# Splits of activations and norms of compressed inputs queued at other places beside the products, in a two-block transformer kernel on one core

## What is computed

```python
# first block, after the mixer
x = x + m[2] * rms_norm(y, norm_mix_post)
f = swiglu(modulate(rms_norm(x, norm_ffn_pre), m[3], m[4]), w_gate, w_up, w_down)
x = x + m[5] * rms_norm(f, norm_ffn_post)
...
# second block, each of two layers
h = rmsnorm(h_res, norm_gain[l])
proj = h @ w_in[l]            # u_pool, z_pool, c_q, c_kv, k_rope, z_mla, g_pool, g_mla
y_pool = (pool_mix(u_pool) * silu(z_pool)) @ pool_w_up[l]
c_q, c_kv = rmsnorm(c_q, g_qa), rmsnorm(c_kv, g_kva)    # 768 and 256 wide
o_mla = attention(c_q @ w_q_b, c_kv @ w_kv_b, k_rope)
y_mla = (o_mla * silu(z_mla)) @ mla_w_up[l]
merged = sigmoid(g_pool) * y_pool + sigmoid(g_mla) * y_mla
h_res = h_res + merged @ w_out[l]
```

## Time and profile before

| | |
|---|---|
| time, median of 3 runs | 3752.34 us (3749.4 to 3755.61) |
| the profiled execution | 3751.09 us, its span 3749.3 us |
| PE busy | 3390.0 us, 90% |
| DVE, ACT, POOL busy | 1957.6, 1434.3, 218.8 us |
| mean granted TensorE clock | 0.936 of full |
| chain that ended last | PE 77%, DVE 14%, ACT 6%, issue 1%, DMA 1% |
| DMA | 321.82 MB, mean 86 GB/s |

### The profile page before, as it was taken

The page is one execution under the profiler, slowest core; times in us unless marked ns, Lnnn a source line. Parts: engine busy times, 40 slices in busy tenths (PEclk is TensorE's granted clock), DMA queues, the critical chain, the costliest instruction groups (busy, mean ns, idle before and its releaser), DMA issues.

```text
span 3749.3 us, 51094 instructions
## 1 busy us (share of the span) xinstructions
PE 3390.0 (90%) x20406; PEld 2828.6 (75%) x20406; DVE 1957.6 (52%) x2838; ACT 1434.3 (38%) x2196; POOL 218.8 (6%) x225
## 2 busy tenths in 40 slices
PE   1998776579999999998998999999999989999998
PEld 1776544467778777878855779999988557799998
DVE  6647577866544444446454544454453645444433
ACT  2532465334432333234245443342342444433322
POOL 1000033210000000000020000000000200000000
PEclk9999876569999999999999999999999989899999
DMA  5562101013333224222200002333432000033333
GB/s 194 181 204 92 46 17 62 3 66 112 107 112 118 94 92 158 96 96 103 81 1 29 24 24 88 108 131 94 136 109 75 1 29 24 24 88 107 116 91 102
DMA packets 94493, 321.82 MB, mean 86 GB/s; under 512 B 10352, under 2 KB 11632, under 8 KB 93488
## 3 DMA queue, kind: packets, MB, share of 16 engines
q1 hardware_dynamic: 76224, 249.66, 20.3%
q0 software_dynamic: 17312, 67.78, 5.1%
q10 hardware_dynamic: 720, 1.12, 0.1%
HBM read 295.38 MB, written 23.20 MB: 85 GB/s over the span
## 4 chain that ended last, share of the span: by engine, by line
PE 77%; DVE 14%; ACT 6%; issue 1%; DMA 1%; DVEq 0%; ACTq 0%; POOL 0%; SPq 0%; POOLq 0%
PE psum L146 74%; DVE mixer L171 4%; PE psum L149 3%; DVE mixer L181 2%; DVE wlo L171 1%; DVE arena L171 1%; DVE junk L185 1%; ACT arena L155 1%; DVE arena L194 1%; ACT whi L163 1%; DVE mixer L198 1%; ACT arena L154 1%; DVE region L171 1%; ACT arena L163 0%; ACT region L163 0%
## 5 line engine op out<-in xcount | busy, mean ns | idle before, releaser
L146 PE MATMUL psum<-region,whi 128*128 128x260 f32 (+2 forms) x8896 | 1909.6, 312 | 28.8 <-DVE region L171 22.3
L146 PEld LDWEIGHTS psum<-region,whi 128*128 128x128 f32 (+1 forms) x8896 | 1443.6, 188 | 138.8 <-issue 28.8
L146 PE MATMUL psum<-region,wlo 128*128 128x260 f32 (+2 forms) x4448 | 1380.2, 310 | 0.0
L171 DVE TENSOR_TENSOR wlo<-stage,whi 128x1024 fp32r<-128x1024 f32 (+2 forms) x454 | 512.7, 1129 | 777.1 <-ACT whi L163 742.1
L146 PEld LDWEIGHTS psum<-region,wlo 128*128 128x128 f32 (+1 forms) x4448 | 839.6, 189 | 49.2
L163 ACT CAST whi<-stage 128x1024 fp32r<-128x1024 f32 (+2 forms) x454 | 441.8, 973 | 272.2 <-PE psum L146 172.8
L146 PE MATMUL psum<-arena 128*128 128x65 f32 (+8 forms) x2064 | 419.5, 354 | 4.1 <-ACT arena L155 2.3
L163 ACT COPY arena<-psum 128x512 f32<-128x512 f32 (+10 forms) x428 | 190.0, 444 | 431.3 <-PE psum L146 397.2
L146 PE MATMUL psum<-mixer 64*128 64x128 f32 (+6 forms) x1140 | 228.5, 443 | 122.5 <-DVE mixer L171 56.3
L146 PEld LDWEIGHTS psum<-arena 128*128 128x128 f32 (+4 forms) x2064 | 253.7, 180 | 101.1 <-issue 90.5
L154 ACT ACTIVATE arena<-psum 128x260 f32<-128x260 f32 (+1 forms) x236 | 100.8, 427 | 598.7 <-PE psum L146 598.0
(11 more groups left out here) (144 smaller groups left out, 2796.4 us busy)
## 6 DMA issues: line engine op xcount, KB each, us to landing
stage<-in_w SPq DMA_DIRECT2D x144, 512.0 KB, 3.5
stage<-in_wi SPq DMA_DIRECT2D x55, 512.0 KB, 4.2
stage<-in_wm SPq DMA_DIRECT2D x48, 512.0 KB, 3.4
stage<-in_wo SPq DMA_DIRECT2D x48, 512.0 KB, 3.4
stage<-in_wg SPq DMA_DIRECT2D x44, 512.0 KB, 3.2
stage<-in_wu SPq DMA_DIRECT2D x44, 512.0 KB, 3.2
stage<-in_wd SPq DMA_DIRECT2D x32, 512.0 KB, 3.3
arena<-xr_scratch POOLq DMA_DIRECT2D x7, 2080.0 KB, 9.1
```

The costliest lines, as they stand in the source:

```text
L146: return Issued(self, self.e and self.e.matmul(out, w, x, start=start, stop=stop, skip_group_check=True))
L171: return Issued(self, e and e.tensor_tensor(out, a, b, op))
```

## The change

It does these things:

- `Halves` can wait for its place row by row (`room(k)`). `h_second` waits for row k of the narrow product instead of the whole one (`pe_gemm` signals each row, `each=True`); `h_mg` waits for its first four rows only for the last but one up product, and DVE makes these four ahead of the last up product's four instructions.
- `hf[0]` waits for the first chunk's last output product, and is queued in the last two steps of the output stage, on DVE between the last four scalings.
- `hf[1]` and `h_in[0]` are steps beside the third part's down products, two per product, no longer at once ahead of them; the squares of the last norm (`END1`) follow them.
- The norm of the compressed inputs of half 0 is queued after `h_second`, beside the second half's products; that of half 1 goes in one product earlier; both have four empty steps before the roots, not two.
- The norms of layer 1's input have other empty steps: `steps(3, 3, 2)` for `(0, 1, 0)` and `steps(9, 6, 0)` for `(7, 4, 0)`.

```diff
-def pe_gemm(e, W, bank, psum, key, name, units, rhs, nch, N, done, count, M=128):
+def pe_gemm(e, W, bank, psum, key, name, units, rhs, nch, N, done, count, M=128, each=False):
...
                 ins = e.matmul(o, wl[:, k, :], xh, False, n == len(units) - 1 and k == nk - 1)
+                if each and ci == nch - 1 and k < nk - 1:
+                    ins.then_inc(*done.up("row", key, k))
             if ci < nch - 1:
...
                 done.mark(key, ci)
+                if each and ci == nch - 1:
+                    done.mark("row", key, nk - 1)
...
 def stages(n, s):
...
     def __init__(self, key, st, hi, lo, src, ready, free, B=None):
-        self.key, self.st, self.hi, self.lo, self.src, self.ready, self.free, self.B = (
-            key, st, hi, lo, src, ready, free, B)
+        self.key, self.st, self.hi, self.lo, self.src, self.ready, self.B = key, st, hi, lo, src, ready, B
+        self.room = free if callable(free) else lambda k: free
...
     def steps(self):
...
 def act_half(e, h, k):
     A = h.st.act
-    for c, s in (*h.ready(k), *h.free):
+    for c, s in (*h.ready(k), *h.room(k)):
         e.wait_ge(*c[s])
...
 def dve_half(e, h, k):
     A, D = h.st.act, h.st.dve
-    for c, s in (*h.ready(k), *h.free):
+    for c, s in (*h.ready(k), *h.room(k)):
         e.wait_ge(*c[s])
...
     hf = [Halves(f"f{ch}", sout, fh, fl, nx[ch], lambda k, ch=ch: [(sout.dve, ("sc", ("pre", ch), k))],
-                 [(sout.pe, (("wo", 1, 7), 0))] if ch == 0 else [(sffn.pe, (("wu", 0, 21), 0))],
+                 [(sout.pe, (("wo", 0, 7), 0))] if ch == 0 else [(sffn.pe, (("wu", 0, 21), 0))],
                  B=mod[:, 24:32]) for ch in range(2)]
...
     LAY0 += n_in[1].scales()
-    END1 = [x for s in n_end1[0].squares() for x in (*GAP, s)]
+    sq = n_end1[0].squares()
+    END1 = [sq[0], sq[1], sq[2], *GAP, *GAP, *GAP, sq[3]]
...
     OUT1 += [added(n_post[0][0], "post", 0, xc, n_pre[0])[a:b] for a, b in ((2, 7), (7, 14), (14, 21))]
-    OUT1 += [[], [("root", n_pre[0], 0), ("rec", n_pre[0], 0)], n_pre[0].scales(), []]
+    sc, hv = n_pre[0].scales(), hf[0].steps()
+    OUT1 += [[], [("root", n_pre[0], 0), ("rec", n_pre[0], 0)], sc[0:4], [x for k in range(4) for x in (hv[k], sc[4 + k])] + hv[4:]]
...
-    def half_now(e, q, h):
-        for k in range(8):
+    def half_now(e, q, h, k0=0, k1=8):
+        for k in range(k0, k1):
             if q == "act":
...
                 bs.flush()
-        half_now(e, "act", hf[0])
...
     def dve_out(e, bs):
...
                 bs.flush()
-        half_now(e, "dve", hf[0])
...
     def pool_out(e, bs):
...
                         lambda ci, k_: (uh[:, k_], ul[:, k_], D["ul", ch, k0 + k_]), 1, 512, T, A if part == 0 else D)
-                bs.tick()
+                bs.tick(2 if part == 2 else 1)
         T.mark("end" if ch else "half")
...
     def act_ffn(e, bs, ch, mid):
...
                     e.copy(yc[ch][:, m], psum[:, bank.of[key, 0], :]).then_inc(*A.up(key, 0))
-                bs.tick()
+                bs.tick(2 if part == 2 else 1)
...
     def dve_ffn(e, bs, ch, mid):
...
                         *D.up(key, 0))
-                bs.tick()
+                bs.tick(2 if part == 2 else 1)
...
     def ffn(q, f, e, bs):
...
             def mid():
                 bs.flush()
-                half_now(e, q, h_in[0] if ch else hf[1])
-                bs.todo += END1 if ch else []
+                bs.todo += (h_in[0] if ch else hf[1]).steps() + (END1 if ch else [])
             f(e, bs, ch, mid)
...
                        (lambda k: [(S1.dve, ("sc", ("next", 1, 1), k))]),
-                       [(slay[l].pe, (("kr", l, 0), 1))]) for l in range(2)]
-    LAYER = [LAY0, n_in1[1].steps(7, 4, 0)]
+                       lambda k, l=l: [(slay[l].pe, ("row", ("kr", l, 0), k))]) for l in range(2)]
+    LAYER = [LAY0, n_in1[1].steps(9, 6, 0)]
...
     def n_lora(l, half):
...
                     lambda k, l=l, half=half: [(slay[l].dve, (("up", l, half, k, 1), 1))],
-                    [(slay[l].pe, (("up", l, half, 7, 1), 1))]) for half in range(2)] for l in range(2)]
+                    lambda k, l=l, half=half: [(slay[l].pe, (("up", l, half, 7, k // 4), 1))])
+             for half in range(2)] for l in range(2)]
     POOLS = [[s for g, wnd in enumerate((2, 4, 8, 16)) for s in
...
+    def lora_steps(l, half):
+        q_, kv_ = LORA[l][half]
+        out = q_.squares() + kv_.squares() + 4 * GAP + [("root", q_, 0), ("root", kv_, 0)]
+        return out + [("rec", q_, 0), ("rec", kv_, 0)] + q_.scales() + kv_.scales()
...
     def rounds(l, half, e, bs, q, do):
...
                     slay[l].act.mark("tail", l, half)
+            if (n, half) == (7, 1):
+                bs.todo += lora_steps(l, 1)
             bs.tick(4)
-            if n == 7:
-                q_, kv_ = LORA[l][half]
-                bs.todo += q_.squares() + kv_.squares() + 2 * GAP + [("root", q_, 0), ("root", kv_, 0)]
-                bs.todo += [("rec", q_, 0), ("rec", kv_, 0)] + q_.scales() + kv_.scales()
         if half == 0:
...
             half_now(e, q, h_second[l])
+            bs.todo += lora_steps(l, 0)
         else:
...
             def do(key, i):
                 if key[0] == "kr":
-                    pe_gemm(e, W, bank, psum, key, f"wk_{l}", [i], rhs, 2, HC, T, A, M=32)
+                    pe_gemm(e, W, bank, psum, key, f"wk_{l}", [i], rhs, 2, HC, T, A, M=32, each=True)
                 else:
...
         elif l == 0:
-            out += n_in1[0].steps(0, 1, 0)
+            out += n_in1[0].steps(3, 3, 2)
         return out
...
     def beside3(l, half):
...
                 dve_weights(e, W, W.last[key] + 2)
+                if (k, z) == (7, 1):
+                    bs.flush()
+                    half_now(e, "dve", h_mg[l][half], 0, 4)
                 for ci in range(2):
...
         bs.flush()
-        half_now(e, "dve", h_mg[l][half])
+        half_now(e, "dve", h_mg[l][half], 4)
         bs.todo += beside3(l, half)
...
             key = ("wo2", l, half, k)
```

## The result

| | before | changed |
|---|---|---|
| time, median of 4 runs each | 3752.69 us (3749.4 to 3755.61) | 3727.88 us (3724.8 to 3728.76) |
| the profiled execution, its span | 3751.09, 3749.3 us | 3728.76, 3727.0 us |
| mean granted clock | 0.936 | 0.936 |

What follows compares the result with a forecast made beforehand. PE, busy 90% of the span, bounds the kernel, so only its waits or low clock cost time. Terms -19.5 -5.1 -1 -3.6 -3.4 +4 = -28.6 from 3751.1 give 3722.5, 1.2 more against the median: 3723 us, range 3708 to 3737.

Steps and rivals of the forecast that it cites:

- Compressed norms, -19.5: Four norms of the compressed inputs: PE's 3.8 us waits before the column sums go and the sums run faster, saving 19.5 us.
- the 11.4 us against 13.6: Behind the compressed norms' sums, reciprocals and weight split end after 11.4 us; PE has work for 13.6, so they stay hidden.
- Split of half 1, layer 0, -5.1 and 0 for the row-wise release: Second token half: layer 0 becomes like layer 1, saving 5.1 us; freeing each row by itself gives 0 in both layers.
- Merged halves, -1: Four splits of the merged rows: DVE ends no sooner, PE waits twice; 1 us gained in all, through the clock.
- The rule weighed there: At the merged halves, shorter waits may leave the clock high at all four sites, giving up to 10 us instead of 1.
- Halves inside the FFN, -3.6: Third part of the down products: halves fit beside the products, removing PE's waits of 2.20 and 1.39 us; 3.6 us saved.
- Input norms of layer 1, -3.4: Column sums of layer 1's two input norms: 2 us saved at the first, about 2 us wait remaining, and 1.4 at the second.
- FFN start, +4: First FFN split: four scalings between the halves make row 7 3.1 us later, plus 0.9 for the clock; 4 us lost.
- the bounds of parts 3, 5 and 6: Merged halves: gain 2.5 to loss 1.5 us a site; first layer-1 input norm: 0 to 4 saved; FFN start: 3 to 6 lost.
- row by row works: Rival: merged halves end near PE's pace, 5.7 us at each of four sites, some 5 at two half changes; 3682 to 3712; chance 0.11.
- A new wait: Rival: PE stalls 3.5 us behind the reciprocals at each of four norms, 14 us in all; 3737 us; chance 0.10.
- slower: Rival: products beside the norms wait 2.2 us for weights, 20 times, 44 us; 3767 us; chance 0.02.

Runs made afterwards that it cites:

- norms alone: Only the compressed-input norms moved, with four empty steps, on the kernel before: 3732.6 us, ratio 0.9945.
- merged halves back: Changed kernel with all eight halves of the merged rows again behind the last up product's own work: 3722.22 us, ratio 0.9921.
- FFN start back: Changed kernel with eight scalings, then eight halves after the last output product, as before the change: 3718.62 us, ratio 0.9917.
- the repeat: The changed kernel itself, unaltered, measured and profiled again: 3731.91 us, ratio 0.9923.
- the early split: Changed kernel with ACT making half 1's eight high halves ahead of its copy of the narrow product's second chunk: 3718.6 us, ratio 0.9915.
- FFN start strictly in turn: Changed kernel with the FFN's first split one output product earlier, each scaling followed by its half: 3733.7 us, ratio 0.9952.

## Why the prediction was right

The time forecast was 3723 us in a range of 3708 to 3737; it is 3728. By parts:

1. *Compressed norms, -19.5.* Right. The three sites that stand alone gave 15.4 us against 14.4 forecast, PE no longer waits for DVE's sums of squares there, and DVE's reciprocals are hidden: they end at 1795.94, the weight split behind them at 1797.30, and PE has no wait, as the 11.4 us against 13.6 had said. With two empty steps the waits were back at all four sums, so the cause is shown.
2. *Split of half 1, layer 0, -5.1 and 0 for the row-wise release.* The wait is 2.05 us, as forecast, and with the norm beside it the site gave 8.3 us of 10.1: the split there loses 7.2 us, where layer 1's old 5.3 had been taken as the model. That the release does nothing as long as ACT copies first was shown twice: the wait is 2.05 us without the release too (norms alone), and with ACT's order turned round 8.6 us came at two sites. The step that was short is "0 us for both layers": layer 1 lost 1.6 us more, at an unchanged wait, because PE's clock was down for longer (0.62 over 8 us, 0.79 before). The forecast took layer 1's old cost for both layers and never asked whether the clock would be the same. Whether the change brings this loss stays open. The same code lost 6.8 us in layer 1 in most profiles and 5.6 in the run with the merged halves back; in layer 0 it lost 7.2 in most, 5.5 with the FFN start back and 5.7 with the merged halves back; and the norms alone, without the release, lost 7.1 in layer 0 and 5.3 in layer 1. The wait was 2.05 us each time, so the wait doesn't set the loss, and the higher loss comes without the release as well.
3. *Merged halves, -1.* The mechanism was right (DVE has no gap behind 2416.58, so its last half ends no sooner), the sign of the remainder wrong: +1.5 by the table. The 1 us of gain was my choice between bounds of -2.5 and +1.5 a site. The idle time did stay the same (0.97 and 2.16 us for 3.00), so the rest is the clock, and it went both ways. At the first site the loss rose from 6.3 to 7.6 us, at the second it fell from 7.8 to 6.7, at the fourth it rose from 6.4 to 7.9 (6.8 in the repeat). The windows that answer to the earlier trace rows, 2.9 us long and 0.3 us behind DVE's last half, at the first two sites:

```profile
2416.38:2419.28 2.90, 2.90 (x14) 2.90 (x15) 1.46 (x2) 0.67 (x2) 0.00 (x0) 0.51 0.70 224
2657.36:2660.26 2.90, 2.90 (x22) 2.90 (x23) 1.47 (x2) 0.67 (x2) 0.00 (x0) 0.86 0.68 207
```

   Before the change it was 26 matmuls at 1.00 at the first site and 14 at 0.50 at the second. So the two waits in place of one left the clock lower at one site and higher at the next, and gained nothing in sum. The rule weighed there (the Trainium skill, page TensorE: Matmul & The Clock Gate, section What's actually happening), that activity releases the clock, did not carry the guess that two shorter waits keep it high at all four sites. That single waits of 0.2 us leave it high is what the run with the early split shows.
4. *Halves inside the FFN, -3.6.* Right: -4.1, no wait left.
5. *Input norms of layer 1, -3.4.* -4.3. The wait that was to remain at 2 us is 1.97:

```profile
2526.74 1.12 PE L146 MATMUL psum<-arena,cst 128*128 128x260 f32 x4 [1.97 <-DVE arena L171]
```

6. *FFN start, +4.* Right: +3.9, 3.1 of it row 7's delay; the clock (granted 1.00 in the first 8 us before, 0.64 now) took its part as well. In two later profiles the same code lost 2 us less, so the exact hit is partly luck.

Of the 3.4 us between -28.6 and -25.2, 2.5 stand in part 3, 1.6 in layer 1's split and 1.8 in layer 0's, less 2.5 that the others gave beyond the forecast. That these misses partly cancel is luck. The rest, from 25.2 to the span's 22.3, is chance in untouched stages. Two of the prediction's sums don't follow from its own terms, without consequence for the result: the bounds of parts 3, 5 and 6 give 3711 to 3734, not 3713 to 3732, and the lower end of row by row is 3723 less four times 5.7 and twice 5, some 3690, not 3682.

Of the rivals, *row by row works* was wrong for this change. Its place was right, though: both waits it named can be shortened by an edit that starts the halves sooner (to 1.5 us and to 0.2), which is what the Trainium skill, page Perfetto Trace Analysis, section Optimization Strategy, asks for (make what a gap waits for start sooner), and which the runs bear out with 13 and 8.6 us. I had weighed that rule against what the change does and found it doesn't start them sooner; had I looked at what stands in front of DVE's 1.22 us weight split, an idle time of 5.56 us, I could have said what would. *A new wait* and *slower* did not come: there is no wait on wlo beside the norms.

## What to carry to other kernels

A steps list with a distance in it (empty steps) is a schedule: one product more between a norm's squares and its column sum gave four fifths of everything here, so look first for sums that wait less than a product's length (3.8 us of 5.7 here). Freeing a buffer row by row does nothing until the engine that writes it gets there sooner; read the row ahead of the first write on each engine, not the semaphore. When a split crosses two engines (scale, high half, low half), keep the scaling some rows ahead, since in lockstep each row pays both hand-overs.

## What the runs showed of the hardware

- After a wait of 2 us in which the inputs then came row by row, PE ran at 1.2 GHz for some of the next matmuls, in amounts that the wait alone doesn't tell: 41 or 31 matmuls in 8 us behind waits of 1.99 and 2.05 us (layer 1, before and changed). Where single stalls stayed at 0.2 us (the split early), the granted clock was 1.00.
- A row handed from DVE to ACT and back costs more than its three operations: 2.4 us for 0.75, 0.72 and 0.75, so 0.06 us a hand-over, all three in series (FFN start strictly in turn); with three rows of lead a row took 1.65 us.
- Stages that a change doesn't touch differ by up to 5 us between profiles of such kernels (554.3 to 559.4), and sites with the same code, most of which repeat to 0.1 us, now and then by 1 to 2 us (the FFN start 12.3 for 14.2, a split 5.6 for 6.8), with unchanged waits at the splits. One span is no evidence for 3 us, and one site none for 1.
